# Four down projections as seven block products instead of eight, combined by VectorE

## The reference, cut to what matters

```python
h = modulate(rms_norm(x, norm_g[layer, 1]), sh2, sc2)
x = x + g2[:, None, :] * (jnp.square(jax.nn.relu(h @ w_ff1[layer])) @ w_ff2[layer])
```

## Time and profile before

| | |
|---|---|
| median of 3 runs | 1365.6 us (1364.85 to 1367.06) |
| span of the profiled execution | 1365.3 us |
| TensorE busy | 1336.1 us (98%) |
| VectorE busy | 656.9 us (48%) |
| ScalarE busy | 466.5 us (34%) |
| GpSimd busy | 195.0 us (14%) |
| mean granted clock of TensorE, share of full | 0.994 |

### The profile page before, as it was taken

One profiled execution on the slowest core, in us unless ns is written; L12 is line 12 of the kernel. 1 busy time (PEld: TensorE's weight loads), 2 busy tenths in 40 slices (PEclk: granted clock), 3 DMA queues, 4 the chain that ended last, 5 costly groups with the idle time before them and its releaser, 6 DMA issues.

```text
span 1365.3 us, 26614 instructions
## 1 busy us (share of the span) xinstructions
PE 1336.1 (98%) x10622; PEld 1248.6 (91%) x10622; DVE 656.9 (48%) x1203; ACT 466.5 (34%) x776; POOL 195.0 (14%) x270
## 2 busy tenths in 40 slices
PE   8899999898999999999999999999999999999997
PEld 6789877787888988988999999999999999999997
DVE  3434332665645633333334653667565343443465
ACT  3433322444233423123224331323344231322354
POOL 4200163962400100001000210003001000000000
PEclk9999999998999999999999999999999999999999
DMA  9977786215564456355322221223224223223242
GB/s 338 369 253 246 231 299 235 71 63 173 200 215 155 157 192 207 93 166 187 123 67 88 94 93 62 66 67 94 88 72 130 72 85 91 92 92 93 65 152 97
DMA packets 128813, 195.70 MB, mean 143 GB/s; under 512 B 5884, under 2 KB 104713, under 8 KB 125652
## 3 DMA queue, kind: packets, MB, share of 16 engines
q1 hardware_dynamic: 112004, 122.83, 28.1%
q0 software_dynamic: 16720, 71.64, 15.1%
HBM read 189.82 MB, written 4.62 MB: 142 GB/s over the span
## 4 chain that ended last, share of the span: by engine, by line
PE 92%; DVE 2%; DMA 2%; issue 2%; ACT 1%; POOL 0%; POOLq 0%; DVEq 0%; SPq 0%; ACTq 0%
PE gemm L1634 76%; PE gemm L2051 3%; PE gemm L1789 2%; PE aux_ps L1669 2%; DMA ada_w<-in_w_ada 1%; PE stat_ps L1801 1%; PE aux_ps L1837 1%; PE stat_ps L1738 1%; PE stat_ps L1979 1%; ACT P L833 1%; DMA v_third<-in_cache_v 1%; PE aux_ps L1719 1%; PE gemm L1938 1%; DVE P L1396 0%; PE aux_ps L1777 0%
## 5 line engine op out<-in xcount | busy, mean ns | idle before, releaser
L1634 PE MATMUL gemm<-h_split,w_hi 128*128 128x272 f32 (+1 forms) x3328 | 569.8, 293 | 4.1 <-DVE w_lo L1013 1.8
L1634 PEld LDWEIGHTS gemm<-h_split,w_hi 128*128 128x128 f32 x3328 | 471.0, 189 | 43.2 <-issue 37.9
L1634 PE MATMUL gemm<-h_split,w_lo 128*128 128x272 f32 (+1 forms) x1664 | 346.8, 290 | 0.0
L1634 PE MATMUL gemm<-hid_split,w_hi 128*128 128x272 f32 x2048 | 340.9, 288 | 0.0
L624 ACT ACTIVATE w_hi<-raw_panels 128x1024 fp32r<-128x1024 f32 x192 | 202.1, 1053 | 307.5 <-PE gemm L1634 304.8
L1634 PEld LDWEIGHTS gemm<-hid_split,w_hi 128*128 128x128 f32 x2048 | 289.5, 188 | 0.0
L1013 DVE TENSOR_TENSOR w_lo<-raw_panels,w_hi 128x1024 fp32r<-128x1024 f32 x192 | 234.5, 1223 | 95.6 <-ACT w_hi L624 94.2
L1634 PEld LDWEIGHTS gemm<-h_split,w_lo 128*128 128x128 f32 x1664 | 263.2, 189 | 0.0
L1634 PE MATMUL gemm<-hid_split,w_lo 128*128 128x272 f32 x1024 | 211.6, 288 | 0.0
L1634 PEld LDWEIGHTS gemm<-hid_split,w_lo 128*128 128x128 f32 x1024 | 160.5, 188 | 0.0
L1027 DVE SCALAR_TENSOR_TENSOR ffv<-gemm,rel 128x544 f32<-128x544 f32 x48 | 34.8, 725 | 174.2 <-ACT rel L644 174.2
(11 more groups left out here) (314 smaller groups left out, 1260.0 us busy)
## 6 DMA issues: line engine op xcount, KB each, us to landing
raw_panels<-in_w_ff SPq DMA_DIRECT2D x68, 1024.0 KB, 5.5
ada_w<-in_w_ada POOLq DMA_DIRECT2D x36, 1024.0 KB, 5.3
kv_ring<-in_cache_k SPq DMA_DIRECT2D x64, 256.0 KB, 3.6
raw_panels<-in_w_in_ab SPq DMA_DIRECT2D x12, 1024.0 KB, 10.5
kv_ring<-in_cache_v POOLq DMA_DIRECT2D x36, 256.0 KB, 4.3
raw_panels<-in_w_in_c SPq DMA_DIRECT2D x8, 1024.0 KB, 5.7
v_third<-in_cache_v POOLq DMA_DIRECT2D x28, 256.0 KB, 4.9
ada_first<-in_w_ada POOLq DMA_DIRECT2D x8, 512.0 KB, 11.8
```

The lines of the kernel that those rows point to most:

```text
L1634: ins = mm(G[slot][:, 512 - T0W * (1 - half):512 + (T0W + rows) * half], w[:, s, k, :], rhs(k, part, T0W * half, T0W + rows * half), start ...
```

## The change

In blocks 1 and 2 of both layers the down projection (4 of 8) is computed pair by pair: a **pair** is the two units of a panel, and its 2 by 2 blocks of weights (row half by column half) and the 2 by 2 blocks of the hidden activations (row half by token half) are multiplied with the Strassen-Winograd scheme: seven products of 4 row chunks by 3 passes over 272 columns (12 matmuls each) in place of eight. That takes, per pair:

- four weight sums on GpSimd (`weight_sums`, 512 elements per partition), and seven high and seven low weight parts of 512 elements (`form_hi` on ScalarE, `form_lo` on VectorE) in place of two of 1024;
- products P1..P7 (k = 0..6) go to banks SB0, SB5, SB1, SB0, SB1, SB5, SB1; the first to enter a bank starts it afresh, the second adds to it. ScalarE copies out P1 and P2 before they are added to (`keep_p1`, `keep_p5`), VectorE makes the shared sums from these copies and adds the four result blocks to `x` (`sum_u2`, `add_c11`, `sum_c22`, `add_c22`, `sum_c12`, `add_c12`, `add_c21`, `add_samples`).

In the up part of those blocks the hidden activations get four sums on GpSimd per two units (`hid_sums`, 272 elements) and six hi/lo forms (b1, t1, b2, t2, t4, t3). The weight sums of pair 0 stand in GpSimd's list after the sums of up unit 3, those of pairs 1 to 3 after the sums of unit 7. The loads of `w_ada` chunks 34 to 47 move from GpSimd's own loop into this list (`load_second`). The three loads for the next stage (`ws_raw`, `gv_row`, `bs_row`) come behind it, the memset of `fin_ss` moves into `ff`, `gate_pm` (gates with signs) is made once per layer, and the blocks of the four engines' lists that were loops over b are written out.

GpSimd:

```diff
+            def weight_sums(B, j, t):
+                G_, p = 4 * B + j, t // 2
+                pool.wait_ge(raw_in[p % 2], 16 * (p // 2 + 1))
+                if G_:
+                    pool.wait_ge(lo_form, LO_FORM0 + 5 * (G_ - 1) + 2)
+                nc.gpsimd.tensor_tensor(w_sum[:, 0, :, :], w_quarter(raw, p, 0, 1), w_quarter(raw, p, 1, 1),
+                                        ALU.add).then_inc(ws_add, 1)
...
+            def fast_block(layer, b):
+                B, T = fast_ix(layer, b), (T_FF1 if layer else T_FF0) + 16 * b
+                for s in range(8):
+                    if layer == 0 and 34 + 8 * (b - 1) + s < 48:
+                        load_second(34 + 8 * (b - 1) + s)
+                    hid_sums(B, s // 2, T + s, s % 2)
+                    if s == 3:
+                        weight_sums(B, 0, T + 8)
+                for j in range(1, 4):
+                    weight_sums(B, j, T + 8 + 2 * j)
```

ScalarE, a form waits for the product of the pair before that used its place:

```diff
+            def form_hi(B, j, k):
...
+                elif k < 5:
+                    act.wait_ge(prod, PROD0 + 5 * (n - 1) + k + 1)
+                else:
+                    act.wait_ge(unit_done, UD0 + t - 6 + k)
```

VectorE's list in the down part (`hid_..._lo(.., 3)` are the last activations of the up part):

```diff
+                hid_t2_lo(4 * B + 3, 3)
+                hid_t4_lo(4 * B + 3, 3)
+                form_lo(B, 0, 6)
+                hid_t3_lo(4 * B + 3, 3)
+                sum_u2(0)
+                add_c11(0)
+                if layer == 0:
+                    ada_turn(3 + b)
+                form_lo(B, 1, 0)
+                form_lo(B, 1, 1)
+                sum_c22(0)
+                form_lo(B, 1, 2)
+                add_c22(0)
+                form_lo(B, 1, 3)
+                sum_c12(0)
+                form_lo(B, 1, 4)
+                add_c12(0)
+                add_c21(0)
+                form_lo(B, 1, 5)
+                add_samples(0)
+                form_lo(B, 1, 6)
+                for j in range(1, 3):
+                    for k in range(3):
+                        form_lo(B, j + 1, k)
+                    sum_u2(j)
+                    add_c11(j)
+                    form_lo(B, j + 1, 3)
+                    sum_c22(j)
+                    form_lo(B, j + 1, 4)
+                    add_c22(j)
+                    sum_c12(j)
+                    form_lo(B, j + 1, 5)
+                    add_c12(j)
+                    add_c21(j)
+                    form_lo(B, j + 1, 6)
+                    add_samples(j)
+                split_next(u)
+                sum_u2(3)
...
```

TensorE's waits in a pair:

```diff
+                    for k, bank in enumerate((SB0, SB5, SB1[j % 2], SB0, SB1[j % 2], SB5, SB1[j % 2])):
...
+                        if k < 2:
+                            pe.wait_ge(psum_free, t + 1)
...
+                        if k == 3:
+                            pe.wait_ge(bank_cp, BANK_CP0 + 2 * n + 1)
+                        if k == 4:
+                            pe.wait_ge(comb, COMB0 + 9 * n + 1)
...
+                        if k == 6:
+                            pe.wait_ge(comb, COMB0 + 9 * n + 4)
```

More of the change, by code:

```diff
@@ L113, in trunk_kernel @@
     slopes = place("slopes", [128, NH])
+    pages_ix = place("pages_ix", [1, 128], i32)
+    ident = place("ident", [128, 128])
+    ones = place("ones", [128, 128])
     rank4 = place("rank4", [128, 4])
@@ L597, in _ @@
+            load_second(32)
+            load_second(33)
+            pool.wait_ge(norm[1]["h"], KC)
+            for b in FAST:
+                fast_block(0, b)
             pool.wait_ge(ada_used, 48)
+            pool.wait_ge(unit_done, UD0 + T_FF0 + 48)
             pool.dma_start(ws_raw[:, :, :], a["w_s"][0].rearrange("g t s -> t g s")).then_inc(ws_in, 16)
@@ new lines, in hid_t4_hi, with hid_t3_hi, fast_up @@
+            def hid_t4_hi(Q, i):
+                act.wait_ge(t_add, T_ADD0 + 4 * Q + 3)
+                A(hid_t4[i][:, 0, :], t4_sum[i][:, 1, :], ACT.Copy).then_inc(hid_hi, 1)
+            def hid_t3_hi(Q, i):
+                act.wait_ge(t_add, T_ADD0 + 4 * Q + 4)
+                A(hid_t3[:, i, 0, :], t3_sum[:, i, 1, :], ACT.Copy).then_inc(hid_hi, 1)
+            def fast_up(layer, b, T):
+                B = fast_ix(layer, b)
+                for s in range(8):
+                    t, i = T + s, s // 2
+                    if s == 7 and layer == 0:
+                        ada_copy(3 + b)
+                    if s < 5:
+                        split_hi(ahead(t // 4, t % 4))
+                    else:
+                        form_hi(B, 0, 2 * (s - 5))
+                        form_hi(B, 0, 2 * (s - 5) + 1)
+                    act.wait_ge(unit_done, UD0 + t + 1)
+                    act.wait_ge(psum_free, t + 2)
+                    A(rel[:, 0, :], gall[s % 2], ACT.Relu).then_inc(relu_r, 1)
+                    if s % 2:
+                        hid_odd_hi(i, t)
+                        continue
+                    if i:
+                        hid_t2_hi(4 * B + i - 1, i - 1)
+                        hid_t4_hi(4 * B + i - 1, i - 1)
+                        hid_t3_hi(4 * B + i - 1, i - 1)
+                    hid_even_hi(4 * B + i, i, t)
@@ L949, in ff @@
                         apply_chunk(1 + 2 * layer, 2 * m + 1)
-                with act.Fori(1, 3) as b:
-                    up(b, True) if ada else up_short(b)
-                    down(b)
+                for b in FAST:
+                    fast_up(layer, b, T0 + 16 * b)
+                    fast_down(fast_ix(layer, b))
                 up_short(3)
@@ L1491, in up_short @@
                         for s in range(4):
[L1492 to L1497, removed]
+                            step_relu(q0 + 4 * b + i, s, J + 8 * b + 4 * i + s, 16 * layer + 8 + 4 * i + s, 4 * i + s)
                 ada = layer == 0
@@ L1516, in ff @@
                     step_resid(q0 + 2 + m // 4, m % 4, R0 + m, m, gate)
-                with dve.Fori(1, 3) as b:
-                    up(b, True) if ada else up_short(b)
-                    down(b)
+                dve.wait_ge(norm[nn]["h"], KC)
+                V.tensor_copy(gate_pm[:, 0:KC:2, :], adaT[:, gate:gate + KC:2, :])
+                V.tensor_scalar(gate_pm[:, 1:KC:2, :], adaT[:, gate + 1:gate + KC:2, :], -1.0, None, ALU.mult).then_inc(gate_rdy, 1)
+                dve.wait_ge(gate_rdy, GATE_RDY0 + layer + 1)
+                for b in FAST:
+                    fast_up(layer, b, T0 + 16 * b)
+                    fast_down(layer, b)
                 up_short(3)
@@ L2085, in ff @@
                     ada_turn(3)
-                down(0)
+                first_down()
                 pe.wait_ge(norm[nn]["h"], KC)
-                with pe.Fori(1, 3) as b:
+                for b in FAST:
                     up_ada(b) if layer == 0 else up(b)
-                    down(b)
+                    fast_down(fast_ix(layer, b))
                 up(3)
```

327 lines of the change are left out of this document (288 added, 39 removed).

## The result

The changed kernel takes **1385.0 us** (median of 4, 1382.3 to 1389.9), the kernel before 1365.2 us beside it: ratio 1.0148, 95% interval 1.0126 to 1.017. It is slower by 19.8 us, on the side and inside the range predicted; the 1394 was 9 us too high.

A forecast was written before the change was run, and what follows sets the result against it. TensorE was taken to bound the kernel before, GpSimd and VectorE excluding one another the changed down blocks. Adding 24.0 (four blocks) and 4.8 (`w_ada` chunks) to 1365.3 gave 1394 us; range for all 1360 to 1409.

The forecast's parts named there:

- TensorE's saving: Down blocks: 84 matmuls a pair in place of 96 save 6.03 us a block, 24.1 us over four.
- Exclusion of GpSimd and VectorE: Down blocks: GpSimd sums and VectorE's two-SBUF-input instructions exclude one another, 11.1 us in a pair of 10.55.
- The rival of sums running side by side: Down blocks: GpSimd's weight sums and VectorE run beside each other, stalls some 1.0 us a block; 1346 us, chance 0.16.
- The block walk: One down block followed pair by pair: stalls of 12.0 less 6.03 saved, 6.0 us longer a block, 24.0 for four.
- up to four sums: Block's pair 2: VectorE's same list meets up to four GpSimd sums, partly beside PSUM-reading instructions; 2.5 us lost with `keep_p1`'s wait.
- That P7 of pair 0 waits 1.1: Down block, pair 0: `sum_c22` ends at 13.3 us where P7 wanted it at 12.3, a 1.1 us stall.
- The bound of 48.4 us a block: Down blocks: 37.8 us of mutually exclusive work in pairs 0 to 2 plus 10.55 for pair 3; no shorter while exclusion holds.
- The memset of `fin_ss`: Up parts: under half a us on VectorE while TensorE runs a unit of 6 us; put at nothing.
- The chunks of `w_ada`: Layer 0 up parts: `load_second(38)` and 46 stand behind pair 0's sums; two waits of 2.4 us, 4.8 in all.
- The clock: TensorE's clock drops after stalls: 0 to 3 us a block, 1.7 a chunk, 15 in all; taken as 0.
- the rival of 1409: Stalls also bring down TensorE's clock and TensorE pays: 1394 + 15 = 1409 us, chance 0.10.
- Packed without loss (1368): Down blocks: exclusive time packs without loss, blocks 48.4 us at best, sum 0 to +5; 1368 us, chance 0.16.

The follow-up runs named there:

- the kernel with early sums on VectorE: Changed kernel with VectorE's list reordered, pairs 1 to 3 weight sums on VectorE, fifth `w_ada` load ahead, third and fourth sums moved earlier: 1345.0 us, ratio 0.9851.
- the kernel with the load ahead: Changed kernel with the fifth `w_ada` load of the two layer 0 blocks issued before pair 0's weight sums: 1381.8 us, ratio 1.0123.
- the repeat: The changed kernel unchanged, run once more beside the first experiments: 1383.7 us, ratio 1.0135.
- the kernel that only writes: Changed kernel with each GpSimd weight sum replaced by a memset of all of `w_sum`, forms reading panel quarters: 1363.1 us, ratio 0.9979.

## Why the prediction was right, point by point

**TensorE's saving: right.** It stands in the kernel with early sums on VectorE: 5.2 to 5.5 us a block of the 6.03 predicted.

**Exclusion of GpSimd and VectorE: right, and shown.** Taking the 64 sums away (1348.6), leaving them unread (1384.6) and turning them into writes (low parts back at 728 ns) leaves one of the readings weighed here: GpSimd's reads against VectorE's second SBUF input. The assumption that instructions reading PSUM are not held up, taken as 0, holds: 430 ns for `sum_u2`'s first half beside the sums and 432 without them. The rival of sums running side by side falls; its time, 1346, is within 3 us of the kernel without sums.

**The block walk: its mechanism right, its size 2 us a block too big.** That is the term that was mis-sized: 24.0 predicted for four blocks, 15.6 measured; with the 2.0 of the chunks, and less the 0.6 of the memset, it is the difference between the sum of 28.8 and the 19.0 of the account. Pair by pair in the block shown, predicted against measured: pair 0 17.65 and 16.42, pair 1 12.75 and 13.73, pair 2 13.05 and 11.52, pair 3 10.75 and 10.83. In pair 0 P5 stalled 2.34 in place of 3.2 (1.90 to 2.34 over the four blocks), and the start of pair 1 1.64 in place of 2.7: the walk had GpSimd and VectorE strictly take turns from the beginning, while VectorE's first low parts had to wait for ScalarE anyway and the first sums of 272 ran beside that. In pair 2 the step "up to four sums" failed: two were left (the 2.10 us of GpSimd in the third row of the stretches), the other two had run in pair 1, which is therefore longer. The walk also left out that the smallest SBUF instruction can pay a whole sum: `s_tmp`, 64 elements, took 768 ns on average where it takes 217 without the sums.

**That P7 of pair 0 waits 1.1: half of it, and in two blocks of four.** There it waited 0.54 and 0.55. In the other two TensorE had fallen to a slower clock after the P5 stall (below), so that P7 came late by itself.

**The bound of 48.4 us a block: not contradicted.** In the kernels in which GpSimd makes all weight sums, with the list of before or another, the blocks take 51.7 to 53.2.

**The memset of `fin_ss`: put at nothing, cost 0.6.** The forecast looked at the time it takes on VectorE (0.09 us), not at what stands behind it in ScalarE's list.

**The chunks of `w_ada`: right in place and count, too long.** Two waits, of 1.4 and 1.3 us in place of 2.4: the load was issued at 633.14, 10.6 us after unit 3 ended, not 11.5, as three of four sums there met nothing and took 1.3. In the kernel with the load ahead both up parts are at 57.2 us again; its median is 1.9 us lower, about the 2.8 that its waits lost.

**The clock: taken as 0, and it cost next to nothing.** After the 2.34 us stall the granted clock is low for the next product (busy time by stretch, PEclk third from last):

```profile
1125.50:1129.20 3.70, 3.70 (x19) 3.70 (x19) 3.70 (x6) 0.75 (x2) 2.31 (x3) 0.54 0.65 223
```

0.54 is nearly the lower of the two levels (1.2 GHz) throughout, as after the 1.78 us wait of before, 0.71. In this block P5 to P7 took 6.3 us in place of 4.5. But the start of pair 1 then still waits 1.64 for VectorE, which had no gap meanwhile (3.70 of 3.70 us in this row); at full clock that wait would have been longer by the same. Two executions of the same block bear that out, layer 0 block 1 in the repeat and in the changed kernel's profile:

```profile
543.11:595.30 52.19, 43.86 (x340) 42.37 (x338) 44.86 (x73) 21.04 (x38) 20.98 (x15) 1.00 0.26 82
...
541.43:593.59 52.16, 45.39 (x340) 43.90 (x338) 44.50 (x73) 20.91 (x38) 20.79 (x15) 0.97 0.25 81
```

At full clock throughout (the first row) TensorE waited more; where the clock fell once (the second) it was busy longer and waited less; the block took 52.2 us both times. So the rival of 1409 falls; no row had given its 3 us a block or 1.7 a chunk, and the two chunks were followed by a granted clock of 1.00. That a lower clock costs where no later wait takes it up is seen in the kernel that only writes. The length of a stall alone does not tell what the clock does: in that block of the repeat stalls of 1.91 and 2.31 us left it at 1.00.

**Packed without loss (1368): no.** The blocks' 52 us lie between its 48.4 and the forecast's 54.

**Against the median.** The sum was set against a span; the early stretch differs by up to 7 us from one profile to the next, which no term covered and the range did.

## What to carry to other kernels

Before moving elementwise work to an idle GpSimd, look in the trace whether VectorE's neighbours in time have both inputs in SBUF: then a sum costs its own, longer time on both engines, and may be cheaper on the "busy" VectorE. While two engines exclude one another and together fill the stage, rearranging their lists gains nothing; once they don't, two sums that stood three and four places too late cost 8.6 us. Follow a wait through every engine's list before moving something: the copy that TensorE waited for could have run, but stood behind a form that couldn't. An instruction of 0.09 us that changes its place in a list can hold up by over 1 us the engine that waits for it.

## What the runs showed of the hardware that was not expected

- The smallest instruction can pay a whole wait: a VectorE product of 64 elements took 768 ns on average beside GpSimd's sums and 217 without them, while a sum of the same size a few places behind it stayed at 219.
- A GpSimd memset of 1.81 us leaves VectorE's two-input instructions at 728 ns; reading sums of 1.4 to 1.5 us bring them to 860 and 1022.
- VectorE adds 512 elements in 0.69 us, GpSimd in 1.3 where it meets nothing.
- In one block of the changed kernel a stall of 2.34 us brought the granted clock to 0.54 over the next 3.7 us, and stalls of 1.23 to 1.64 left it at 1.00; in a block of the repeat a stall of 2.31 left it at 1.00 too.
